# A 32-byte gap between the feature rows of a three-layer transformer kernel

## The reference

```python
def rms_norm(x, w=None):
    xf = x.astype(jnp.float32)
    y = xf * lax.rsqrt(jnp.mean(xf * xf, axis=-1, keepdims=True) + EPS)
    ...
def swiglu(h, w_gate, w_up, w_down):
    return (jax.nn.silu(h @ w_gate) * (h @ w_up)) @ w_down
...
        m_lat = adaln_params(c, w_ada[i], b_ada[i])
        ...
        a_lat = modulate_2(rms_norm(h_lat), m_lat[0], m_lat[1])
        ...
        h_lat = h_lat + m_lat[2] * o_lat
        h_lat = h_lat + m_lat[5] * swiglu(modulate_2(rms_norm(h_lat), m_lat[3], m_lat[4]),
                                          w_ffn_gate[i], w_ffn_up[i], w_ffn_down[i])
```

## Time and profile before

| | |
|---|---|
| time, median of 3 runs | 1456.03 us (1455.59 to 1456.46) |
| span of the profiled execution | 1454.6 us |
| TensorE matmuls, busy | 1403.6 us (96%), 8272 records |
| TensorE weight loads, busy | 1172.3 us (81%) |
| VectorE busy | 848.5 us (58%) |
| GpSimd busy | 840.2 us (58%) |
| ScalarE busy | 659.0 us (45%) |
| HBM read | 238.50 MB, 165 GB/s over the span with what is written |

### The profile page before, as it was taken

One profiled execution on the slowest core, in us unless ns is written; L12 is line 12 of the kernel. 1 busy time (PEld: TensorE's weight loads), 2 busy tenths in 40 slices (PEclk: granted clock), 3 DMA queues, 4 the chain that ended last, 5 costly groups with the idle time before them and its releaser, 6 DMA issues.

```text
span 1454.6 us, 21621 instructions
## 1 busy us (share of the span) xinstructions
PE 1403.6 (96%) x8272; PEld 1172.3 (81%) x8272; DVE 848.5 (58%) x1638; ACT 659.0 (45%) x1070; POOL 840.2 (58%) x672
## 2 busy tenths in 40 slices
PE   5999999999999999999999999999999999999998
PEld 2978789999988888546878888888888866888887
DVE  3798667776676689688675333321126768554522
ACT  3555665455453133684342232232226386544442
POOL 1533427998864444675444554544446530699997
PEclk9999999999999999999999999999999999999999
DMA  9748516777775652010445555533333320365664
GB/s 365 288 164 309 195 50 212 248 258 241 243 259 194 202 192 80 31 44 15 174 174 182 195 202 185 193 122 96 102 107 102 110 94 16 118 200 188 187 187 135
DMA packets 71207, 242.01 MB, mean 166 GB/s; under 512 B 7488, under 2 KB 12992, under 8 KB 70720
## 3 DMA queue, kind: packets, MB, share of 16 engines
q1 hardware_dynamic: 68688, 236.63, 48.1%
q10 hardware_dynamic: 2416, 4.00, 0.9%
HBM read 238.50 MB, written 1.05 MB: 165 GB/s over the span
## 4 chain that ended last, share of the span: by engine, by line
PE 52%; DVE 4%; ACT 1%; issue 0%; POOL 0%; DVEq 0%; ACTq 0%
PE bank L731 9%; PE bank L737 9%; PE bank L732 9%; PE bank L593 8%; PE bank L594 4%; PE bank L584 2%; PE bank L586 1%; PE bank L585 1%; PE bank L592 1%; PE cond_a L1124 1%; PE bank L1124 1%; DVE h_both L2239 1%; PE bank L1132 1%; PE cond_a L1185 1%; PE bank L1144 1%; PE cond_b L1144 1%
## 5 line engine op out<-in xcount | busy, mean ns | idle before, releaser
L2010 POOL TENSOR_TENSOR w_lo<-raw,w_hi 128x512 fp32r<-128x512 f32 (+2 forms) x610 | 776.8, 1302 | 581.1 <-ACT w_hi L1466 572.9
L1466 ACT ACTIVATE w_hi<-raw 128x1024 fp32r<-128x1024 f32 (+3 forms) x300 | 307.9, 1029 | 582.7 <-PE bank L737 375.2
L731 PE MATMUL bank<-h_both,w_hi 128*128 128x512 f32 (+1 forms) x1000 | 323.1, 340 | 1.2 <-ACT w_hi L1466 1.2
L732 PE MATMUL bank<-h_both,w_hi 128*128 128x512 f32 (+1 forms) x1000 | 322.5, 340 | 0.0
L731 PEld LDWEIGHTS bank<-h_both,w_hi 128*128 128x128 f32 x1000 | 188.3, 188 | 22.9 <-ACT w_hi L1466 1.4
L732 PEld LDWEIGHTS bank<-h_both,w_hi 128*128 128x128 f32 x1000 | 188.3, 188 | 21.3
L737 PE MATMUL bank<-h_both,w_lo 128*128 128x512 f32 (+1 forms) x1000 | 198.1, 340 | 0.0
L737 PEld LDWEIGHTS bank<-h_both,w_lo 128*128 128x128 f32 x1000 | 160.4, 188 | 21.4 <-POOL w_lo L2010 0.2
L2124 DVE CUSTOM_DVE_ANT_0 ada_junk<-ada_w,cond_a 128x1024 bf16<-128x1024 f32 x128 | 153.5, 1215 | 15.1 <-DVE work L2687 8.1
L2106 DVE TENSOR_TENSOR hidden_both<-work,hidden_both 128x256 fp32r<-128x256 f32 (+1 forms) x66 | 58.5, 886 | 135.0 <-ACT hidden_both L1547 135.0
L593 PE MATMUL bank<-h_both,w_hi 128*128 128x512 f32 x345 | 122.8, 394 | 0.0
(11 more groups left out here) (487 smaller groups left out, 2544.1 us busy)
## 6 DMA issues: line engine op xcount, KB each, us to landing
raw<-in_up SPq DMA_DIRECT2D x132, 512.0 KB, 3.6
ada_w<-in_ada SPq DMA_DIRECT2D x128, 512.0 KB, 4.5
raw<-in_down SPq DMA_DIRECT2D x48, 448.0 KB, 3.5
raw<-in_out SPq DMA_DIRECT2D x24, 512.0 KB, 3.5
raw<-in_down SPq DMA_DIRECT2D x24, 512.0 KB, 3.6
raw<-in_in SPq DMA_DIRECT2D x24, 512.0 KB, 3.5
arena<-in_ada SPq DMA_DIRECT2D x16, 512.0 KB, 11.8
raw<-in_uq SPq DMA_DIRECT2D x12, 384.0 KB, 3.1
```

Of the source, the lines that this page charges most:

```text
L731: pe.matmul(out, w_h[:, k - k0], hi[:, k, cols], start=(k == 0), stop=False)
L732: pe.matmul(out, w_h[:, k - k0], lo[:, k, cols], start=False, stop=False)
L1466: act.activation(part_slot(w_hi, f, u), raw_slot(f, u), ACT.Copy).then_inc(s["rounded"], 1)
L2010: pool.tensor_tensor(part_slot(w_lo, f, u)[:, a:b], raw_slot(f, u)[:, a:b], part_slot(w_hi, f, u)[:, a:b].bitcast(F32), ALU.subtract).then ...
```

## The change

A constant `ROW_GAP` of 8 elements (32 bytes) is added. `h_both` is declared with rows of 520 columns, and the kernel uses the first 512 of each: a row takes 2080 bytes, of which 32 are never touched. `scratch` grows by as much, and the offsets inside it are moved to where rows begin now. The 512 bytes that this takes in each partition come from the descriptor scratch, which goes from 2048 to 1024 bytes.

```diff
+ROW_GAP = 8
...
-        with nc.sbuf_tensor("scratch", [P, 2 * KD * TOK], F32) as scratch:
+        with nc.sbuf_tensor("scratch", [P, 2 * KD * (TOK + ROW_GAP)], F32) as scratch:
             pass
-        h_both = sbr("h_both", [P, 2, KD, TOK])
+        h_rows = sbr("h_both", [P, 2, KD, TOK + ROW_GAP])
+        h_both = h_rows[:, :, :, 0:TOK]
         h_hi, h_lo = h_both[:, 0], h_both[:, 1]
...
-        ea = [rows3(v) for v in (t1_flat[:, 0:1536], scratch[:, 6144:7680], scratch[:, 2048:3584],
+        ea = [rows3(v) for v in (t1_flat[:, 0:1536], scratch[:, 6240:7776], scratch[:, 2080:3616],
                                  t1_flat[:, 3072:4608], t1_flat[:, 4608:6144])]
...
-        sn_sum, sn_one = scratch[:, 3584:4096], scratch[:, 7680:8192]
+        sn_sum, sn_one = scratch[:, 3616:4128], scratch[:, 7776:8288]
...
-    nc = bacc.Bacc("TRN2", target_bir_lowering=False, num_devices=1, dynamic_dma_scratch_size=2048)
+    nc = bacc.Bacc("TRN2", target_bir_lowering=False, num_devices=1, dynamic_dma_scratch_size=1024)
```

## The result

| | before | after |
|---|---|---|
| time, median of 4 runs each | 1456.12 us (1455.59 to 1456.46) | 1463.34 us (1461.64 to 1466.26) |
| ratio | | 1.0050, 95% interval 1.0036 to 1.0064 |
| span of the profiled execution | 1454.6 us | 1459.8 us |

The kernel is 7.2 us slower. The prediction had the direction right; the size it named, +11.0 us, was too large, and the rule it stood on, that rows must start on a 64-byte boundary, did not hold.

A forecast was written before the change was run, and what follows sets the result against it. TensorE, busy 1403.6 of 1454.6 us, was taken to bound the kernel through the distances between matmul starts; terms 10.8 + 1.3 - 1.1 = +11.0 us gave 1467.0 us, range 1450 to 1470 (the forecast's own 1464 to 1470).

The forecast's parts named there:

- Term 1: 512-column matmuls of L731, L732 and L737: all 1632 lose their short start-to-start distance, 6.6 ns each, +10.8 us.
- the first rival: Feature rows: only odd ones pay, even ones recover the short distance at once; +5.5 us, 1461.5 us, chance 0.20.
- Term 2: 384 512-column matmuls of L584 to L586 and L767 to L772, half counted at 6.6 ns: +1.3 us.
- Term 3: 816 256-column matmuls, with unshifted latents or features as weights, go from 120.0 to 118.6 ns: -1.1 us.
- Term 4: Shifted 256-column products (up0, out0): taken as 0, bounds 0 and +0.9 us.
- Term 5: Matmul pairs of L593/L594 and L591/L592, 345 + 51: taken as 0, bounds -0.2 and +0.2 us.
- Terms 6 and 7: Other rows, FP32 products and other engines' work (sixth), and the smaller descriptor scratch (seventh): 0 each.
- Only the odd rows pay: Feature rows: even rows find the short distance again at once, halving the first three terms; 1461.5 us, chance 0.20.
- The offset doesn't matter: Feature rows: the offset within 64 bytes has no effect, so the gap does nothing; 1456.0 us, chance 0.18.
- The skew rival: Row changes in the feature matmuls: later row starts save up to 3.3 ns each; -7.9 us, 1448.1 us, chance 0.20.
- second beat: TensorE's matmul stream: might settle into a pattern over several rows with an unseen mean, making the whole forecast wrong.

The follow-up runs named there:

- shift32: Kernel before with 1024-byte scratch, no gap, and 32 unused bytes ahead of the features, moving all sixteen rows alike: 1466.39 us, ratio 1.0072.
- shift64: Kernel before with 1024-byte scratch, no gap, and 64 unused bytes ahead of the features: 1459.03 us in one run.
- slots: Kernel before with 1024-byte scratch, features in place modulo 512 bytes, rounded weights moved by 64 bytes per slot, low ones 96 further: 1468.31 us, beside 1460.21 before.
- gap64: The changed kernel with a gap of 64 bytes between feature rows in place of 32: 1463.63 us, ratio 1.0050.
- halves32: Kernel before with 1024-byte scratch and one 32-byte gap, between the eight high and eight low feature rows: 1462.06 us in one run.
- all32: Kernel before with 1024-byte scratch, no gap, and 32 unused bytes ahead of everything, weights included: 1451.32 us in one run.
- scratch_only: Kernel before with only the descriptor scratch cut from 2048 to 1024 bytes, no row gap: 1455.33 us, ratio 0.9991.
- shift256: Kernel before with 1024-byte scratch, no gap, and 256 unused bytes ahead of the features: 1455.66 us in one run.

## Why the prediction was right, and where not

**That the distances decide, and no wait.** Right: +8.5 us of distances, no new wait of note, the control (512 columns of `hidden_both`) unmoved.

**Term 1, the 1632 matmuls of L731 to L737.** This is the mis-sized one. Predicted 6.6 ns each, +10.8 us; measured 5.4, 4.3 and 6.1 ns by line, 544 × 15.8 = +8.6 us. The 6.6 ns of the earlier trace rows is the price of place 32 alone: `uv` has its moving rows 32 bytes behind its weights within 256, and shift32 puts all features there and gets the same 233.3. The gap spreads the rows over all eight places. Their constant-place values in the runs (226.7 before; 233.3 in shift32; 228.9 in shift64; 232.8, 232.5, 233.0, 233.4 and 232.2 in slots, for 96 to 224) have a mean of 231.6 ns, and 232.0 was measured. For gap64, which goes round 0, 64, 128 and 192, the same mean is 230.4, and 230.3 was measured. The mean is all that this explains: row by row the pattern doesn't follow the place (k = 0 of L734 has 224.6, k = 4 237.4). And halves32, by its places 228.9, had 230.0.

**The rule behind term 1** was that a row is off its beat when it doesn't start on a 64-byte boundary, so only odd rows would change. Wrong twice: gap64 keeps all rows on such boundaries and loses the beat, all32 takes all off them and keeps it. In its place the runs show a dependence on the distance between moving row and weight block modulo 256 bytes, with the one good place at 0, of the eight in steps of 32 bytes, for 512 columns. The direction came out right because the prediction compared two operands ("one operand off it") and every changed place but 0 costs something. That the size came near is luck: 6.6 ns, read at one place, was put on all rows by a rule that doesn't hold, and seven of the eight places happen to cost 2 to 7 ns. The time alone would not have told: 1463.3 us is nearer to the first rival's 1461.5 than to 1467.0.

**That the stream doesn't find its beat again between two rows**, which made term 1 count the even rows too, isn't borne out as a general rule. In halves32 the beat is back on the first matmul behind a low row, in the first slot of slots it takes five. The reading of the earlier trace rows behind it was too coarse: in nanoseconds the five distances from 109.76 us take 1.133 us, 226.6 each, so the stream was at its beat there and not on the way to it.

**Term 2**, +1.3 us for the 384 others: measured +0.8 (L586 to L588) and +0.5 (L769, L770, L774), +1.3.

**Terms 3 to 5.** Term 3, -1.1: about -1.0 (vrb 118.5, as written). Term 4, 0: within 0.3 us by line. Term 5, 0: +0.5, a pair 349.2. Since the 256-column distances of one layout differ by 1 ns between profiles, these hits are worth less than they look.

**Terms 6 and 7**, 0: no wait for another engine has grown by more than 1.1 us, and scratch_only settles the seventh.

**The sum.** +11.0 forecast for the profiled execution, +5.2 found: of the 5.8 between them 2.2 are term 1 and 3.3 clock and pauses, which differ between executions of one kernel. The terms as measured add up to 9.4 us; with them belongs -0.5 us of the 256-column products of `hidden_both`, whose rows the change leaves alone and which went from 118.2 to 117.3 ns between the two profiles. The repeat of the changed kernel has 1463.6 in place of 1459.8 with the same distances. The medians, which level some of that out, differ by 7.2 and, in the repeat, 8.0 us, near the 8.5 of the distances.

**The rivals.** "Only the odd rows pay" falls: the even rows' mean is 231.3 ns, the odd ones' 232.6. "The offset doesn't matter" falls. The Trainium skill's page "SBUF — State Buffer", section "Specifications (TRN2)", has 16-byte lines; shifts of 32, 64 and 128 bytes, whole numbers of lines, cost 6.6, 2.2 and about 6 ns here, so that line isn't the unit that matters in these runs. The skew rival has one grain of truth: single distances of 224.6 and 226.0 do occur (L734), but others pay for them, and in no run has a 512-column line a mean under 226 ns. The "second beat", which the prediction named as what would make it wrong, is what happened: a pattern over 24 matmuls. Its mean, 232.0 ns, is between those of the earlier trace rows (231.4) and the earlier trace rows (233.3), so as a size it was less foreign than the prediction feared.

## What to carry to other kernels

When TensorE streams without pauses, read the distance from start to start, not the record's length, and read it for every form: a few nanoseconds on 1632 matmuls are the whole result here. Padding rows of a moving operand is not harmless. In this kernel full rows of a multiple of 256 bytes, at the weights' own place modulo 256, were the best layout tried for 512-column float32r products. One constant bad place cost more a matmul (shift32, 233.3 ns) than rows spread over all places (232.0); in time the two can't be told apart (+0.7% and +0.5%, with intervals that overlap). A control within the kernel that shows a price (here `uv`) should be asked which of its differences makes it: an experiment that moves both operands together would have shown at once that the boundary was not it.

## What the runs showed of the hardware

- The distance of 512-column float32r matmuls by the place of the moving row against the weight block, modulo 256 bytes: 226.7 ns at 0; 228.9 at 64; 233.3 at 32; 232.2 to 233.4 at 96, 128, 160, 192 and 224, these five over stretches of 8 or 16 matmuls (slots). Moving both operands by 32 (all32), or one by 256 (shift256), changes nothing: 226.7. Why is open: a meeting of the next weight load with the moving read would fit a rule that depends on both addresses, but nothing here shows it, and no run changed when the load is made. The loads' own records don't differ: in up1 all but one per unit last 187 to 192 ns and begin 2 to 4 ns behind the start of the matmul ahead, with the place at 0 (before, all32), 32 (shift32) or 64 (shift64) or changing (the kernel after, slots).
- With places that change from matmul to matmul the stream falls into a pattern that repeats unit by unit (a row's distances scatter by 0.3 to 2.0 ns about its mean) and is the same in two executions of the changed kernel.
- For 256 columns the order is another: 120.0 at 0 (the earlier trace rows and the unshifted latents), 118.6 or 117.5 at 160, 117.5 to 115.9 at 192, where pairs of 2 x 256 rise from 348 to 353. Whoever tunes these has to measure several executions.
